# Local attention of a two-block model: row sums of the weights by a column of ones in the values, and the sinks of two heads exponentiated together

## What is computed

```python
scores = einsum('bnqhgd,bnkhd->bnhgqk', qb, kb) * (ATTN_HEAD_DIM ** -0.5)
scores = where(mask, scores, NEG)
m = maximum(max(scores, axis=-1), s)              # s: the head's sink
p = exp(scores - m)
probs = p / (sum(p, axis=-1) + exp(s - m))
out = einsum('bnhgqk,bnkhd->bnqhgd', probs, vb)
```

## Times and profile before

| | |
|---|---|
| median of 3 runs | 3371.64 us (3371.37 to 3372.16) |
| the profiled execution | 3372.35 us, span 3370.6 us, granted clock of PE 0.997 |
| PE busy | 3316.9 us, 98% of the span |
| DVE busy | 1938.0 us, 57% |
| POOL busy | 1471.0 us, 44% |
| ACT busy | 1399.8 us, 42% |
| the units of the local attention | about 219 to 492 us of the span |

### The profile page before, as it was taken

One profiled execution on the slowest core, in us unless ns is written; L12 is line 12 of the kernel. 1 busy time (PEld: TensorE's weight loads), 2 busy tenths in 40 slices (PEclk: granted clock), 3 DMA queues, 4 the chain that ended last, 5 costly groups with the idle time before them and its releaser, 6 DMA issues.

```text
span 3370.6 us, 43537 instructions
## 1 busy us (share of the span) xinstructions
PE 3316.9 (98%) x15738; PEld 2733.5 (81%) x15738; DVE 1938.0 (57%) x2454; ACT 1399.8 (42%) x2422; POOL 1471.0 (44%) x996
## 2 busy tenths in 40 slices
PE   8999999999999999999999999999999999999999
PEld 7778888888888887777888888887888888778887
DVE  6666762854444587784375444457745546535455
ACT  6446660544444436764144445545423324112011
POOL 1121114467777730024346777773534435223340
PEclk9999999999999999999999999999999999999999
DMA  5010012322333331111232233332111111111241
GB/s 217 20 44 17 18 41 100 137 100 100 106 107 119 113 141 41 47 47 70 75 137 99 102 125 113 111 115 108 51 50 62 37 62 50 57 44 62 100 149 63
DMA packets 70968, 283.18 MB, mean 84 GB/s; under 512 B 8048, under 2 KB 12656, under 8 KB 61328
## 3 DMA queue, kind: packets, MB, share of 16 engines
q1 hardware_dynamic: 60176, 236.35, 19.9%
q10 hardware_dynamic: 10624, 44.63, 3.6%
HBM read 249.23 MB, written 30.41 MB: 83 GB/s over the span
## 4 chain that ended last, share of the span: by engine, by line
PE 84%; DVE 6%; issue 3%; ACT 3%; POOL 2%; DMA 0%; ACTq 0%; DVEq 0%; SPq 0%; POOLq 0%
PE G L1062 37%; PE AUX L1469 13%; PE G L1532 10%; PE G L1556 4%; PE G L1805 3%; PE G L1301 2%; PE AUX L1684 2%; PE AUX L1582 2%; PE AUX L1363 2%; POOL slot_lo L890 1%; PE AUX L1430 1%; PE AUX L1353 1%; PE G L1184 1%; PE AUX L1343 1%; PE G L1124 1%
## 5 line engine op out<-in xcount | busy, mean ns | idle before, releaser
L1062 PE MATMUL G<-Hhi,whi 128*128 128x512 f32 x1552 | 631.6, 407 | 7.4 <-DVE Hlo L3062 2.8
L841 POOL CAST whi<-wraw 128x1024 fp32r<-128x1024 f32 (+1 forms) x123 | 135.8, 1104 | 1104.1 <-PE G L1062 593.9
L1062 PE MATMUL G<-Hlo,whi 128*128 128x512 f32 x1552 | 605.6, 390 | 0.0
L1062 PE MATMUL G<-Hhi,wlo 128*128 128x512 f32 x1552 | 605.6, 390 | 0.0
L1062 PEld LDWEIGHTS G<-Hhi,whi 128*128 128x128 f32 x1552 | 292.1, 188 | 74.5 <-issue 7.1
L1062 PEld LDWEIGHTS G<-Hlo,whi 128*128 128x128 f32 x1552 | 292.3, 188 | 62.7 <-issue 5.7
L1062 PEld LDWEIGHTS G<-Hhi,wlo 128*128 128x128 f32 x1552 | 291.8, 188 | 61.9
L843 POOL TENSOR_TENSOR wlo<-wraw,whi 128x1024 fp32r<-128x1024 f32 (+1 forms) x123 | 307.0, 2496 | 9.9
L890 POOL TENSOR_TENSOR slot_lo<-raw_even,slot_hi 128x512 fp32r<-128x512 f32 x156 | 207.9, 1333 | 120.1 <-ACT slot_hi L2189 118.5
L890 POOL TENSOR_TENSOR slot_lo<-raw_odd,slot_hi 128x512 fp32r<-128x512 f32 x156 | 204.6, 1315 | 102.8 <-ACT slot_hi L2189 102.8
L3286 DVE TENSOR_TENSOR X<-G,X 128x1024 f32<-128x1024 f32 x120 | 146.7, 1223 | 142.5 <-PE G L1532 142.5
(11 more groups left out here) (547 smaller groups left out, 8083.5 us busy)
## 6 DMA issues: line engine op xcount, KB each, us to landing
wraw<-wjobs SPq DMA_DIRECT2D x148, 512.0 KB, 3.2
b_hi<-operand_tiles SPq DMA_DIRECT2D x60, 512.0 KB, 6.4
b_lo<-operand_tiles SPq DMA_DIRECT2D x60, 512.0 KB, 7.1
raw_even<-up_units SPq DMA_DIRECT2D x14, 1024.0 KB, 4.8
raw_odd<-up_units SPq DMA_DIRECT2D x14, 1024.0 KB, 4.8
raw_even<-down_units SPq DMA_DIRECT2D x12, 1024.0 KB, 4.7
raw_odd<-down_units SPq DMA_DIRECT2D x12, 1024.0 KB, 4.7
mw_raw<-wjobs SPq DMA_DIRECT2D x16, 512.0 KB, 5.0
```

The lines of the kernel that those rows point to most:

```text
L841: pool.tensor_copy(whi[:, par, 0:kt], wraw[:, par, 0:kt]).then_inc(w_hi, 1)
L1062: mm = pe.matmul(G[:, par if psum is None else psum, cols], w[:, par, k, :], x[:, k, cols], start=(i == 0 and j == 0), stop=(i == kt - 1 a ...
```

## The change

- `vals` gets a column of ones behind the 64 columns of each group, so the last column of weigh's result is the sum of the exponentials. Weigh has 65 columns, and its two heads lie 65 columns apart in the bank.
- ACT's exponential of the scores sums nothing any more.
- DVE's `peak` of an odd unit gets a subtraction at its end, for both heads: negm minus the negated sink, into `wstat`. It waits for its own negm first.
- ACT takes the exponential of that for both heads in one operation, `sinks`, without a bias. It stands in exp of the next even unit, ahead of the exponential of the scores; for the last pair it stands in the last step ahead of the copy.
- `scale_out` adds the sum from PSUM and the sinks. Its wait for weigh now stands ahead of the addition and the reciprocal.
- The values are copied in four operations of 64 columns of each token block instead of two of 128, after a memset of the ones. Three buffers behind `vals` move by 128 bytes.

```diff
--- before.py
+++ after.py
@@ -422,15 +422,15 @@
         keys_hi = sb("keys_hi", [P, KV, S], F32R, U_AT)
         keys_lo = [sb(f"keys_lo{j}", [P, S], F32R, at) for j, at in enumerate(
             (U_AT + 48 * KB, U_AT + 52 * KB, U_AT + 60 * KB, X_AT + 12 * KB))]
-        rotating = sb("rotating", [P, S // 2], F32, U_AT + 24 * KB)
-
-
-        partners = sb("partners", [P, S // 2], F32, U_AT + 26 * KB)
+        rotating = sb("rotating", [P, S // 2], F32, U_AT + 24 * KB + 128)
+
+
+        partners = sb("partners", [P, S // 2], F32, U_AT + 26 * KB + 128)
         partners_k = sb("partners_k", [P, S], F32, U_AT + 56 * KB)
-        vals = sb("vals", [P, NBLK, KV * HD], F32, U_AT + 16 * KB)
+        vals = sb("vals", [P, NBLK, KV, HD + 1], F32, U_AT + 16 * KB)
         cos = sb("cos", [P, S], F32, X_AT)
         sin = sb("sin", [P, S], F32, X_AT + 4 * KB)
-        wmask = sb("wmask", [P, 3 * P], F32, U_AT + 28 * KB)
+        wmask = sb("wmask", [P, 3 * P], F32, U_AT + 28 * KB + 128)
         probs = sb("probs", [P, 2, 3 * P], F32, X_AT + 8 * KB)
 
         lw = sb("lw", [P, 2, 4, P], F32, U_AT)
@@ -1360,8 +1360,8 @@
                         pe.wait_ge(s["os"], v // 2)
                     k0, k1 = key_blocks(v)
                     for t in range(k1 - k0):
-                        mm = pe.matmul(AUX[:, 3, h * HD:(h + 1) * HD], probsT[:, v % 2, t * P:(t + 1) * P],
-                                       vals[:, k0 + t, p // 2 * HD:(p // 2 + 1) * HD], start=(t == 0), stop=(k0 + t == k1 - 1))
+                        mm = pe.matmul(AUX[:, 3, h * (HD + 1):(h + 1) * (HD + 1)], probsT[:, v % 2, t * P:(t + 1) * P],
+                                       vals[:, k0 + t, p // 2, :], start=(t == 0), stop=(k0 + t == k1 - 1))
                     mm.then_inc(s["pv"], 1)
 
                 def turn_result(n):
@@ -2084,6 +2084,11 @@
                     query_raw(0, c)
                 queries_high(0, 0)
 
+                def sinks(n):
+
+                    t = slice(2 * n % 8, 2 * n % 8 + 2)
+                    act.activation(wstat[:, 3, t], wstat[:, 2, t], ACT.Exp)
+
                 def exp(v):
                     if v >= 2:
                         act.wait_ge(s["pt"], v - 1)
@@ -2092,10 +2097,10 @@
                     wait_apart(act, s["mx"], v + 1)
                     t = slice(v % 8, v % 8 + 1)
                     negm = wstat[:, 1, t]
-                    act.activation(wstat[:, 3, t], vcol("sinks", v // 16 * 2 + v % 2), ACT.Exp, bias=negm)
+                    if v and v % 2 == 0:
+                        sinks(v // 2 - 1)
                     e = probs[:, v % 2, 0:width(v)]
-                    act.activation(e, e, ACT.Exp, bias=negm, scale=SINK_SCALE, accum_out=wstat[:, 2, t])\
-                       .then_inc(s["pr"], 1)
+                    act.activation(e, e, ACT.Exp, bias=negm, scale=SINK_SCALE).then_inc(s["pr"], 1)
 
                 def copies(v):
                     act.wait_ge(s["pt"], v + 1)
@@ -2113,6 +2118,9 @@
                     p, u = v // 16, v % 16
                     if v + 1 < U:
                         exp(v + 1)
+                    else:
+                        act.wait_ge(s["mx"], U + 1)
+                        sinks(U // 2 - 1)
                     copies(v)
                     if v >= 3 and v % 2:
                         result((v - 3) // 2)
@@ -2872,11 +2880,14 @@
                         for at in (own, other):
                             dve.tensor_tensor(keys_lo[2 * n + h][at, :], buf[part, 0, :], keys_hi[part, 2 * n + h, :],
                                               ALU.subtract).then_inc(k_lo, 1)
+                dve.memset(vals[:, :, :, HD:HD + 1], 1.0)
                 for n, psum in enumerate((AUX[:, 0:2, :], AUX[:, 2:4, :])):
                     dve.wait_ge(vt, n + 1)
-                    dve.tensor_tensor(vals[:, :, n * P:(n + 1) * P], psum.rearrange("p a (b n) -> p (a b) n", n=P),
-                                      rtok[:, 0, :].rearrange("p (b a) -> p b a", a=1).broadcast_to([P, NBLK, P]), ALU.mult)\
-                       .then_inc(vcopied, 1)
+                    for h in range(2):
+                        half = psum.rearrange("p a (b n) -> p (a b) n", n=P)[:, :, h * HD:(h + 1) * HD]
+                        ins = dve.tensor_tensor(vals[:, :, 2 * n + h, 0:HD], half,
+                                                rtok[:, 0, :].rearrange("p (b a) -> p b a", a=1).broadcast_to([P, NBLK, HD]), ALU.mult)
+                    ins.then_inc(vcopied, 1)
 
                 def own(p, c):
 
@@ -2928,18 +2939,24 @@
                                                         1.0, -3e38, ALU.add, ALU.max, mx))
                     sink = neg_sinks[:, 2 * p + h:2 * p + h + 1]
                     dve.tensor_scalar(negm, mx, -SINK_SCALE, sink, ALU.mult, ALU.min).then_inc(s["mx"], 1)
+                    if h:
+                        both = slice(v % 8 - 1, v % 8 + 1)
+                        dve.wait_ge(s["mx"], v + 1)
+                        above = dve.tensor_tensor(wstat[:, 2, both], wstat[:, 1, both], neg_sinks[:, 2 * p:2 * p + 2], ALU.subtract)
+                        if v == U - 1:
+                            above.then_inc(s["mx"], 1)
 
                 def scale_out(n):
                     dve.wait_ge(s["pr"], 2 * n + 2)
+                    dve.wait_ge(s["pv"], 2 * n + 2)
                     t = slice(2 * n % 8, 2 * n % 8 + 2)
                     total, inv = wstat[:, 2, t], wstat[:, 4, t]
-                    chain.link(dve.tensor_tensor(total, total, wstat[:, 3, t], ALU.add))
+                    weighed = AUX[:, 3, 0:2 * (HD + 1)].rearrange("p (h d) -> p h d", h=2)
+                    chain.link(dve.tensor_tensor(total, weighed[:, :, HD:HD + 1].rearrange("p h a -> p (h a)"), wstat[:, 3, t], ALU.add))
                     chain.link(dve.reciprocal(inv, total))
-                    dve.wait_ge(s["pv"], 2 * n + 2)
                     if n >= 2:
                         dve.wait_ge(s["ot"], n - 1)
-                    dve.tensor_tensor(O_sb[:, n % 2, :].rearrange("p (h d) -> p h d", h=2),
-                                      AUX[:, 3, 0:P].rearrange("p (h d) -> p h d", h=2),
+                    dve.tensor_tensor(O_sb[:, n % 2, :].rearrange("p (h d) -> p h d", h=2), weighed[:, :, 0:HD],
                                       inv.rearrange("p (h a) -> p h a", a=1).broadcast_to([P, 2, HD]), ALU.mult)\
                        .then_inc(s["os"], 1)
```

## The result

The changed kernel takes 3374.30 us (median, 3373.68 to 3382.19); the kernel before, run beside it on the same chip, 3371.51 us (3367.68 to 3375.01). The ratio is 1.0012, with a 95% interval from 1.0007 to 1.0018: 2.8 us, or 0.12%, slower. The profiled execution lasts 3374.82 us, with a span of 3373.0. Forecast were 3376.2 us and a change of less than the 0.2% that the text held a measurement could tell. The interval leaves out 1, so 20 executions of each kernel told a smaller change than that.

The account below looks back on a forecast made before the run. PE was taken to set the pace for most of the stage, with DVE and ACT late only in places. Terms 3.0 + 1.4 + 0.4 - 0.4 - 0.3 + 0.38 = +4.5 us gave a median of 3376.2, eight-in-ten range 3370.5 to 3381.5.

Parts of the forecast that it names:

- First halves: First half of rotating the next pair's queries, pairs 2 to 7: PE delayed 0.5 each, 3.0 us in all, ends 1.4 and 4.5.
- Second halves: Second half of rotating the next pair's queries, pairs 2 to 5: 0.35 each, 1.4 us in all, ends 0.4 and 2.0.
- Last halves: 450 to 464 us: addition may escape POOL's cast, ACT gains, the subtraction costs 0.24 twice; -0.4 us, ends -0.8 and +0.8.
- Pair 1: 230 to 251 us, five odd units in one backlog: +0.7 on DVE, -0.3 by ACT; +0.4 us, ends -0.3 and +1.0.
- copy-bound turns: 250 to 257 us, turns where PE waits for ACT's copy of the weights: -0.3 us, ends -0.6 and 0.
- The end: Last result: addition and reciprocal now behind the wait for weigh, +0.38 us; at the one before, PE's last turning covers it.
- PE's idle time: Sign that the steps are right: PE idle near 20 us from 216 to 493 us, 15.2 before.
- Rival 1: The subtraction comes between POOL's casts and head everywhere, under the DVE-POOL lock; 8.7 us, 3380 to 3381; chance 0.26.
- Rival 4: Change does nothing on PE's path, DVE's slack covers all but the end; 3371 to 3373 us; chance 0.13.
- Rival 2: PE's waits for ACT's copies shrink, additions leave POOL's lock, POOL ends sooner in ten middle halves; -7.1, 3364.5; chance 0.06.
- Rival 3: Added waits bring PE's clock down in the ten middle halves too; +13 on +4.5, 3389 us; chance 0.05.

Follow-up runs that it names:

- Column_with_reading: Changed kernel without the subtraction and joint exponential, the sum from the 65th column, ACT still making an unused sum; ratio 0.9995 to the kernel before.
- column_again: Second profile, unaltered, of the changed kernel without the subtraction and joint exponential; stage from first scores to last turn_result 270.08 us, 271.92 in the kernel before.
- pair_alone: Changed kernel with ACT taking the row sum again and the addition reading it from SBUF, the 65th column unused; 3379.0 us, ratio 1.0022 to the kernel before.
- subtract_later: Changed kernel with the subtraction moved between masked maximum and negm of the next even unit; 3373.7 us, ratio 1.0007 to the kernel before.
- subtract_behind_head: Changed kernel with the subtraction moved to the end of DVE's step, behind own, partner or head; ratio 1.0009 to the kernel before.
- Subtract_twice: Changed kernel with the subtraction made a second time, waiting for the first; ratio 1.0029 to the kernel before.
- column_alone: Changed kernel without the subtraction and joint exponential, each sink exponentiated by itself, the sum still from the 65th column; ratio 1.0003 to the kernel before.
- after: The changed kernel itself, against the kernel before; 3374.30 us, ratio 1.0012.
- column_sink_late: Changed kernel without subtraction and joint exponential, each unit's sink exponentiated before ACT waits for the next negm; 3369.95 us, ratio 0.9997 to the kernel before.

## Why the prediction was right, and where its sizes were off

**Right in its steps.** The 65th column cost nothing: 275 ns, and starts 0.112 us apart as before. The PSUM source cost nothing: 0.149 us, with 0.15 for two SBUF sources before. The Trainium skill (VectorE: DVE Perf Modes, the section on the TRN2 errata) gives fixed costs by which the PSUM source would take 0.065 us more, an estimate from its 120 and 58 cycles that the prediction had weighed. Here page and measurement differ, and the measurement decides. The values and the memset cost nothing: from the second pair's copy to the first scores it is 10.53 us in both kernels (208.56 to 219.09, 206.74 to 217.27). The two copies take 1.29 us instead of 1.23, and partner then waits 0.33 us for its DMA instead of 0.41. PE's waits for O_sb grew and those for the copies shrank, as told.

**First halves: mechanism right, upper end off.** The text left open whether head gets in front of POOL's second cast (0.24) or not (0.75), and took 0.5. The cast goes first, as the 1.28 us of POOL and the 1.03 of head show, and yet the price is 0.48 (results 13, 29, 37, 51); six of them make the 3.0 us of the forecast. Counted from POOL's start, head ended after 281.11 + 0.69 - 280.47 = 1.33 us before and ends after 280.13 + 1.03 - 279.34 = 1.82 now: 0.49 later. (The text had the first cast end within 0.02 us of the subtraction's start; by its own rows, 281.11 and 281.08, it is 0.03.) The upper end had 0.75 because it let head take its whole 0.69 us and a handover after the second cast. Head ends 0.54 us after the cast (280.62 to 281.16), 0.15 less than its usual 0.69; so some of its length had passed while it waited.

**Second halves: too dear.** 0.35 each was forecast, 0.17 is measured (result 17, and likewise 25, 33, 41). The first term, +0.2 at own, came to nothing. Own was held before as well, and ended 0.55 us after POOL's subtraction; now the subtraction of two elements is let go first, and own ends 292.73 - 292.10 = 0.63 after it. But these 0.08 us are gone by the rotation: POOL's casts begin 5.71 us after the start of POOL's subtraction in both kernels (290.33 to 296.04, 289.72 to 295.43). The second term, "up to another 0.25" at head, is the whole price. Counted from the start of the casts, head ended after 296.73 + 1.13 - 296.04 = 1.82 us before and ends after 296.74 + 0.69 - 295.43 = 2.00 now: it was held itself, and now it starts only when the held subtraction is through.

**Last halves: right in mechanism, too small.** -0.4 was forecast, with ends of -0.8 and +0.8; -1.19 came in both profiles of the changed kernel. Column_with_reading has -3.94, with PE's clock at 1.00 from 450 to 470 us, where it was 0.91 before. At that same 0.91 column_again has -3.13. So the freed addition is worth about 3 us, and more where the clock doesn't fall. The subtraction gives 1.9 of it back at equal clock (-1.19 against -3.13): at 462.40 it waits for POOL, and result 54 has a pause of 0.24. The -0.5 for "POOL's subtraction may come sooner" was the wrong quantity. What counts is that head gets in front of it and is spared 1.73 us (2.42 to 0.69), and that PE then stands for 0.57 instead of 2.58 us.

**Pair 1: not to be settled by one profile.** +0.4, and -0.3 for the copy-bound turns, were forecast. With the granted clock of 230 to 260 us at 0.94 in both kernels the change costs +0.52; with 0.83 in both it costs 0.69 - 0.59 = +0.10. The two terms can't be told apart in this.

**The end.** The last turn_result comes 0.34 later against the one before it, 0.38 was forecast. Another 0.24 us had come before that (results 58 to 62), which the text held to be covered.

**PE's idle time.** "Near 20 us" from 216 to 493 us is wrong: 277 - 262.82 = 14.2 in the first profile and 277 - 260.38 = 16.6 in the second, with 15.2 before. A PE at the lower level is busy for longer, so idle time isn't a measure of delay where the clock falls; the starts of one line are.

**Terms that nobody had.** Result 21 loses another 0.28 us, because DVE pauses between the reciprocal and the product, with nothing that it waits for; the changed kernel's timeline:

```profile
315.81 0.17 DVE L2956 RECIPROCAL wstat<-wstat 128x2 f32<-128x2 f32 x1
316.26 0.29 DVE L2959 TENSOR_TENSOR O_sb<-AUX,wstat 128x128 f32<-128x128 f32 x1 [0.28 <-DVE wstat L2956]
```

Both profiles have this pause at the same three products (results 4, 21 and 54), and so have pair_alone, subtract_later and subtract_behind_head, in which DVE has as many instructions. Subtract_twice has it at other products, the kernel before and the column alone at none. There are pauses of the same kind before other operations. The addition of result 46 comes 0.22 us late in all five profiles of these four kernels. The masked maximum ahead of result 38 starts 0.55 us after PE has released it, where 0.18 is usual, and costs that result 0.24; it does so in all of them but subtract_later. The kernel before has such a start ahead of its result 44, in both profiles, and the changed kernel has not, which gives back 0.16. So a pause goes with the place in DVE's instructions and not with chance. Together they make about +0.6 of the 4.2 us of the middle; the ten halves make the other 3.6 (six of 0.48, four of 0.17). What makes the pauses was not tried and stays open.

**Rivals.** Rival 1, the lock in full, is refuted as a sum (8.7 us) and right as a mechanism: the subtraction lasts 0.79 and 1.38 us under it and head 1.03. Rival 4, no effect on PE's path, is refuted by the 4.2 us of the middle, which are there in two executions and in pair_alone, and gone without the subtraction; its time, 3371 to 3373 us, was missed by 1.3. Rival 2, ACT's path wins, would have been right for the column without the subtraction in one place only, the last halves. Rival 3, the clock falls in the ten halves of the middle, didn't come: PE's granted clock is 1.00 in every window from 260 to 440 us. The sum of +4.5 is near the +4.3 of the profile that it was made against, but partly by luck, since its errors offset each other. The last halves were put 0.8 too dear, pair 1 with the copy-bound turns 0.6 and the end 0.2 too cheap. The middle was put at 4.4 and measured 4.2, but its second halves were 0.7 too dear and its pauses of 0.6 were not in the sum. The median moved by only 2.8. The second profile of the kernel before, with a stage 1.4 longer than the base of the sum, shows one way in which that can come about. How often each such fall comes, the runs can't tell, since only profiled ones show it.

## What to carry to other kernels

A small operation that is put on an engine with slack costs nothing in the steady part but does cost where that engine has a backlog: here 0.17 to 0.48 us each in ten places, 3.6 us in all. The price was not its queue time of 0.24 us; it was set by what POOL had running when it came. When it has two SBUF inputs beside a busy POOL, its place matters more than its length, since it changes who of the two goes first; look for the large operation that then stands behind the other engine's. Take two profiles of the kernel before as the base: two parts of the sum could not be forecast here, where the clock falls and where DVE pauses.

## What the runs showed of the hardware

- On DVE an operation of two elements with one PSUM and one SBUF input isn't held by POOL's casts: 0.15 us under the cast of the last halves in five kernels (after, column_alone, column_with_reading, column_sink_late, subtract_behind_head). With two SBUF inputs it is held: 0.45, 0.60, 0.77, 0.79, 1.02 and 1.38 us. The prediction held this possible and showed no row for it. Its trace had one: the product into O_sb, with one PSUM and one SBUF input, takes its usual 0.29 us at 457.80, under POOL's subtraction of 457.63. The Trainium skill (SBUF — State Buffer, Who interferes with whom) names two SBUF inputs as the condition; the trace agrees, 0.15 against 0.77 us for the same addition.
- ACT's exponential of two sinks without a bias pointer takes 0.203 us; that of one sink with the pointer took 0.29.
- Which of POOL and DVE runs first turned on some hundredths of a microsecond. Head that started 0.64 us after POOL's first cast got in front of the second (casts 1.80 us in all); head that started 0.69 after it, in the second halves of before, did not (1.28). Head that came 0.13 us ahead of POOL's subtraction took 0.69 us, 0.05 behind it 2.86.
